# Query and key chunks of sparse attention, cut in quarters over the attention tiles

## The chip, the cores and the metric

One core of a Trainium2 chip. The metric is the device time of one execution in microseconds; the median of three runs of the kernel before is 1286.76 us (1285.74 to 1287.68).

## The reference, cut to what matters

Two transformer blocks on one sequence of 512 tokens with 1024 features. The first (gated mixing, convolution, feed-forward) is not touched. The second has two attentions side by side, and then a feed-forward:

```python
proj = jnp.einsum('bsd,dc->bsc', rmsnorm(x, g_pre_mix), w_in)
(q_a, k_a, v_a, q_i, k_i, w_i, q_d, k_d, v_d) = jnp.split(proj, SPLIT_POINTS, axis=-1)
q_a = apply_rope(q_a.reshape(B, S, DSA_HEADS, HEAD_DIM), cos, sin)
k_a = apply_rope(k_a.reshape(B, S, DSA_HEADS, HEAD_DIM), cos, sin)
...
o_a = dsa_attention(q_a, k_a, v_a, q_i, k_i, w_i)      # 8 heads of 64, each query keeps its top 128 keys
o_d = diff_attention(q1, q2, k1, k2, v_d, lam)         # 4 heads: (softmax(q1 k1) - lam softmax(q2 k2)) v
mix = jnp.concatenate([o_a.reshape(B, S, DSA_W), rmsnorm(o_d, g_diff_sub) * (1.0 - lam_init)], axis=-1)
x = x + rmsnorm(jnp.einsum('bsc,cd->bsd', mix, w_out), g_post_mix)
```

"Sparse attention" is dsa_attention, "differential attention" is diff_attention. The top 128 keys are the same for all eight heads of a query; here they come out of 16 rounds, in each of which the eight largest scores are found and struck out, and become a mask.

## The kernel before, in words

The engines run programs of their own, written out by hand in the order in which each works, and meet at semaphores only. Features lie on partitions, tokens on the free axis.

**Weights.** All weights come from HBM as chunks of 128 x 1024 float32, in one stream (`wstream`, put together in `kernel`, line 1830 on), over four slots. SP reloads a slot when GpSimd has split it (L303). GpSimd splits each chunk into a high part (`high`, L342) and a low part (`low`, L345: a subtraction of two SBUF tensors), when TensorE has done the chunk four before (`chunk_done`). A float32 product is made of three matmuls (`three`, L449 to L452: high by high, high by low, low by high), so a chunk is 8 x 3 matmuls of 128x512 (`chunk_transposed`, L454).

**Tiles.** The attention stage has 48 tiles of 128 queries: tiles 0 to 15 are the four differential heads by four query blocks, tiles 16 to 47 the eight sparse heads by four query blocks. Block tb of a head looks at (tb + 1) x 128 keys, so tiles come in four widths. Each engine has its own `step(n)`. TensorE (L804): scores of tile n+2 (or n+3 in the sparse part) into banks 4 and 5 by turns (`scores`, L726), output pieces, `turn(n)` (L746: transposes of the probabilities), `values(n-1)` (L759). VectorE (L1688): `normalise(n)` (L1666), then `shift(n+2)` (L1651: mask and row extreme). ScalarE (L1121): copy of the turned tile (`keep_turned`, L1098), exp of tile n+2 (L1088), the head's output and its square every fourth tile (`keep_output`, L1109).

**Between the tiles.** The differential heads are normalised by a root over their 128 features. TensorE sums the squares after tiles 5, 9, 13 and 17 (L819), ScalarE takes roots at tiles 9 and 17 (L1136), VectorE builds diagonals (`spread`, L1239) at tiles 10 and 18, and TensorE spreads them over the partitions (`norm_spread`, L537) at the tiles of SPREAD_AT; VectorE then scales the kept head by them (L1698 to L1705). ScalarE makes its high part (HIGH_AT, L1140), GpSimd its low part (L419).

**The sparse queries and keys.** Eight chunks, four of q_a and then four of k_a, are projected from C_QA on. `STEPS_AFTER` (L97) says how many tiles each engine does after each chunk: two after the first, one after each other, so tiles 0 to 8 lie between the chunks, whole chunks each, in banks 0, 1, 2 by turns (L828). Two chunks make a rotary pair (first and second halves of four heads): VectorE's `rope_first` (L1553), `rope_second` (L1563) and `rope_join` (L1568), the last of which adds and subtracts two SBUF tensors. The last pair has a tile between second and join. After each even chunk VectorE does one of the last four top rounds (`top`, L1604), after chunk 6 the mask (L1731). ScalarE moves each finished pair into `qa` or `ka` with eight DMAs in a row (`move_rope`, L1037), after the step of every second chunk (L1162). Nothing but the tiles themselves lies on TensorE from then to tile 21.

**Output pieces.** The second half of the output product, for the differential heads, is cut in 32 pieces of three matmuls (`out2_piece`, L789), one per tile from FILL_FROM = 21 on and two at tiles 26, 30, 34 and 38 (`pieces_at`, L100), in banks 2 and 7. `turn` uses bank 3 in the differential tiles and banks 0 and 3 by turns in the sparse ones.

## Time and profile before

| | us |
|---|---|
| median of three runs | 1286.76 |
| the profiled execution | 1278.78 |
| its span, first to last instruction | 1277.1 |
| TensorE busy in the span | 1204.4 (94%) |
| VectorE busy | 654.9 (51%) |
| GpSimd busy | 703.4 (55%) |
| ScalarE busy | 286.4 (22%) |
| granted TensorE clock, mean over the span | 0.976 of full |

The profile is of one execution. Times on its timeline are us from the span's start. The attention stage runs from about 683 to 862. A matmul's start is what to go by: at a steady rate those of 128x512 start every 0.23 us and are listed with 0.39 us, since they overlap.

### The profile page before, as it was taken

The numbers are of one execution on the slowest core, as the hardware profiler recorded it, in microseconds if no ns is written. First come the engines' busy times: TensorE is split into PE (matmuls) and PEld (weight loads), VectorE is DVE, ScalarE is ACT, GpSimd is POOL, SyncE is SP. The second block draws the span as 40 slices with busy tenths as digits, with TensorE's granted clock in tenths as the row PEclk, the third lists the DMA queues.
The fourth block names the chain that finished last, engine by engine and source line by source line (L and its number), as shares of the span: only waits on it lengthen the run. The fifth ranks groups of instructions, "written<-read, shape, count | busy, mean of one in ns | idle before, by whom it ended". The sixth has DMA issues, their size and how long they took to land.

```text
span 1277.1 us, 15445 instructions
## 1 busy us (share of the span) xinstructions
PE 1204.4 (94%) x5310; PEld 948.4 (74%) x5310; DVE 654.9 (51%) x1011; ACT 286.4 (22%) x553; POOL 703.4 (55%) x421
## 2 busy tenths in 40 slices
PE   7999778999999999999999989998899999999995
PEld 5877556888888888877676755666688888888883
DVE  4996956551015534467996775435755100444114
ACT  5153133220002211110202245444231000221011
POOL 6866336666666666655554421214586666666652
PEclk9999979999999999999999989999899999999997
DMA  6321102333222222224332320001032222323201
GB/s 239 130 83 64 52 31 102 99 99 99 96 91 93 98 99 99 99 91 132 99 99 83 99 83 1 20 31 66 17 132 95 91 93 99 99 99 99 99 17 66
DMA packets 34319, 111.23 MB, mean 87 GB/s; under 512 B 4704, under 2 KB 4832, under 8 KB 34272
## 3 DMA queue, kind: packets, MB, share of 16 engines
q1 hardware_dynamic: 29520, 103.30, 24.1%
q10 hardware_dynamic: 4752, 7.31, 2.1%
q8 instruction: 29, 0.48, 0.2%
q14 instruction: 18, 0.15, 0.0%
HBM read 102.99 MB, written 2.10 MB: 82 GB/s over the span
## 4 chain that ended last, share of the span: by engine, by line
PE 84%; DVE 11%; issue 2%; ACT 1%; ACTq 1%; POOL 1%; DMA 0%; DVEq 0%; POOLq 0%
PE bank L450 24%; PE bank L451 23%; PE bank L452 23%; PE bank L779 2%; PE bank L743 2%; DVE bank L1315 2%; PE bank L481 2%; PE bank L483 2%; PE bank L482 2%; DVE ss L1223 1%; PE bank L540 1%; PE bank L756 1%; DVE work L1595 1%; ACTq L1043 1%; DVE xl L1229 1%
## 5 line engine op out<-in xcount | busy, mean ns | idle before, releaser
L345 POOL TENSOR_TENSOR wl<-raw,wh 128x1024 fp32r<-128x1024 f32 x188 | 457.8, 2435 | 15.7
L342 POOL TENSOR_SCALAR wh<-raw 128x1024 fp32r<-128x1024 f32 x188 | 203.7, 1083 | 459.6 <-PE bank L452 348.6
L450 PE MATMUL bank<-xh,wh 128*128 128x512 f32 x840 | 338.8, 403 | 17.6 <-DVE xl L1229 8.8
L451 PE MATMUL bank<-xl,wh 128*128 128x512 f32 x840 | 330.0, 393 | 0.0
L452 PE MATMUL bank<-xh,wl 128*128 128x512 f32 x840 | 329.9, 393 | 0.0
L450 PE MATMUL bank<-uh,wh 128*128 128x512 f32 x576 | 227.3, 395 | 6.0 <-DVE ul L1338 3.1
L451 PE MATMUL bank<-ul,wh 128*128 128x512 f32 x576 | 224.7, 390 | 0.0
L452 PE MATMUL bank<-uh,wl 128*128 128x512 f32 x576 | 224.7, 390 | 0.0
L450 PEld LDWEIGHTS bank<-xh,wh 128*128 128x128 f32 x840 | 159.3, 190 | 69.6 <-issue 24.5
L452 PEld LDWEIGHTS bank<-xh,wl 128*128 128x128 f32 x840 | 159.3, 190 | 33.9
L451 PEld LDWEIGHTS bank<-xl,wh 128*128 128x128 f32 x840 | 159.7, 190 | 32.5 <-issue 1.4
L1482 DVE TENSOR_TENSOR ul<-tmb,uh 128x512 f32 x64 | 123.7, 1932 | 90.2 <-ACT uh L1017 90.2
L1016 ACT ACTIVATE tmb<-tmp 128x512 f32<-128x512 f32 x64 | 40.5, 633 | 418.6 <-DVE tmp L1479 418.6
L450 PEld LDWEIGHTS bank<-uh,wh 128*128 128x128 f32 x576 | 108.7, 189 | 32.2 <-issue 6.0
L451 PEld LDWEIGHTS bank<-ul,wh 128*128 128x128 f32 x576 | 108.7, 189 | 23.1 <-issue 0.9
L452 PEld LDWEIGHTS bank<-uh,wl 128*128 128x128 f32 x576 | 108.5, 188 | 22.8
L1479 DVE SCALAR_TENSOR_TENSOR tmp<-bank,rb 128x512 f32<-128x512 f32 x64 | 44.1, 690 | 82.1 <-PE bank L452 71.9
L1315 DVE SCALAR_TENSOR_TENSOR bank<-gpad,cols,bank 128x512 f32<-128x512 f32 x108 | 73.2, 752 | 0.0
L1493 DVE TENSOR_TENSOR x<-bank,x 128x512 f32 x8 | 5.5, 692 | 78.1 <-PE bank L452 78.1
L1495 DVE COPY y<-bank 128x512 f32 x8 | 5.5, 692 | 78.1 <-PE bank L452 78.1
L1500 DVE TENSOR_TENSOR y<-bank,y 128x512 f32<-128x512 f32 x8 | 5.5, 692 | 72.3 <-PE bank L452 72.3
L481 PE MATMUL bank<-wh,xh 128*128 128x512 f32 x96 | 39.1, 408 | 3.0 <-DVE tmb L1210 3.0
(217 smaller groups left out, 1151.1 us busy)
## 6 DMA issues: line engine op xcount, KB each, us to landing
raw<-wstream SPq DMA_DIRECT2D x189, 512.0 KB, 3.3
x<-xT SPq DMA_DIRECT2D x8, 256.0 KB, 5.9
out<-x SPq DMA_DIRECT2D x8, 256.0 KB, 2.1
qi<-ropey ACTq DMA_DIRECT2D x16, 64.0 KB, 2.2
qd<-ropey ACTq DMA_DIRECT2D x16, 64.0 KB, 2.5
kd<-ropey ACTq DMA_DIRECT2D x16, 64.0 KB, 2.0
qa<-ropey ACTq DMA_DIRECT2D x16, 64.0 KB, 2.1
ka<-ropey ACTq DMA_DIRECT2D x16, 64.0 KB, 2.1
```

What stands on the lines that cost most here:

```text
L342: nc.gpsimd.tensor_scalar(wh[c][:], raw[c][:], 1.0, 1.0, ALU.mult, ALU.mult).then_inc(high_ready, 1)
L345: nc.gpsimd.tensor_tensor(wl[c][:], raw[c][:], wh[c][:].bitcast(F32), ALU.subtract).then_inc(split_ready, 1)
L450: mm(out, wh_, mh, start=start, stop=False)
L451: mm(out, wh_, ml, start=False, stop=False)
L452: return mm(out, wl_, mh, start=False, stop=stop)
L481: mm(out, xh[:, k, ts], wh[s][:, ws], start=k == 0, stop=False)
L482: mm(out, xh[:, k, ts], wl[s][:, ws], start=False, stop=False)
L483: last = mm(out, xl[:, k, ts], wh[s][:, ws], start=False, stop=k == 7)
L1016: A(tmb[c][:], tmp[c][:], ACT.Square).then_inc(square_ready, 1)
L1315: ins = V.scalar_tensor_tensor(out=out, in0=src, scalar=w, in1=acc, op0=ALU.mult, op1=ALU.add)
L1479: V.scalar_tensor_tensor(out=tmp[c][:], in0=bank[c][:], scalar=0.0, in1=rb[:], op0=ALU.max, op1=ALU.mult).then_inc(evacuated, 1)
L1482: V.tensor_tensor(ul[:, bass.ds(r * 4 + c, 1), :].rearrange("p a n -> p (a n)"), tmb[c][:], uh[:, bass.ds(r * 4 + c, 1), :].rearrange("p a ...
```

## The change

The chunks of q_a and k_a come by groups of four heads: two of q_a, two of k_a, then the other two of each (C_QK). Each chunk is cut in four quarters of six matmuls, and `quarters_at(n)` gives the quarters that TensorE does at the head of its step n: two at tiles 0 to 7, one at tiles 8 to 19, and two at 9, 12, 15 and 18. The chunks use banks 0 and 2 by turns, and a semaphore of their own, `qk_out`, counts VectorE's readings of them. VectorE does rope_first after its step of the tile that ends an even chunk (1, 5, 10, 16), and rope_second and rope_join together after that which ends an odd one (3, 7, 13, 19); the top rounds come after steps 0, 2, 4 and 6, the mask after step 9. ScalarE issues two rotary DMAs after each of four steps, from tiles 4, 8, 14 and 20 on. TensorE asks for the first two pairs' DMAs before the scores of tile 16 and for all before those of tile 32. `turn` alternates banks only from tile 22 on. HIGH_AT goes from tiles 18, 19, 20, 22 to 20 to 23, and the output pieces begin at tile 23 in place of 21, with two at 25, 28, 31, 34, 37 and 40.

```diff
--- before.py
+++ after.py
@@ -67,9 +67,8 @@
 C_KD = C_QD + 4
 C_VD = C_KD + 4
 C_VA = C_VD + 4
-C_QA = C_VA + 4
-C_KA = C_QA + 4
-C_OUT2 = C_KA + 4
+C_QK = C_VA + 4
+C_OUT2 = C_QK + 8
 C_FF2 = C_OUT2 + 8
 CHUNKS = C_FF2 + 4 * FH
 
@@ -79,8 +78,7 @@
 E_P2 = E_FF1 + 2 * FH
 E_VD = E_P2 + 13
 E_VA = E_VD + 4
-E_QA = E_VA + 4
-E_OUT2 = E_QA + 8
+E_OUT2 = E_VA + 4
 E_FF2 = E_OUT2 + 16
 
 
@@ -88,13 +86,34 @@
 
 DIFF_TILES = DIFF_HEADS * TB
 TILES = DIFF_TILES + HEADS * TB
-FILL_FROM = 21
+FILL_FROM = 23
+ALTERNATE_FROM = 22
 
 
 SPREAD_AT = {11: 0, 12: 1, 19: 2, 21: 3}
-HIGH_AT = {18: 0, 19: 1, 20: 2, 22: 3}
+HIGH_AT = {20: 0, 21: 1, 22: 2, 23: 3}
 OUT2_BANKS = (0, 6, 2, 3)
-STEPS_AFTER = (2, 1, 1, 1, 1, 1, 1, 1)
+ROUNDS_AT = (0, 2, 4, 6)
+MASK_AT = 9
+MOVES_FROM = {4: 6, 8: 7, 14: 8, 20: 9}
+
+
+def quarters_at(n):
+
+
+    if n < 0 or n >= 20:
+        return range(0)
+    if n < 8:
+        return range(2 * n, 2 * n + 2)
+    doubled = (9, 12, 15, 18)
+    first = 8 + n + sum(d < n for d in doubled)
+    return range(first, first + 1 + (n in doubled))
+
+
+def turn_bank(n):
+
+    return 0 if n >= ALTERNATE_FROM and n % 2 == 0 else 3
+
 
 
 def pieces_at(n):
@@ -102,7 +121,7 @@
 
     if n < FILL_FROM:
         return range(0)
-    doubled = (26, 30, 34, 38)
+    doubled = (25, 28, 31, 34, 37, 40)
     first = n - FILL_FROM + sum(d < n for d in doubled)
     return range(first, first + 1 + (n in doubled))
 
@@ -276,7 +295,7 @@
         scores_done, shifted, exp_done, probs_ready, turned, pT_ready, pv_done, o_kept = (
             sem("scores_done"), sem("shifted"), sem("exp_done"), sem("probs_ready"), sem("turned"),
             sem("pT_ready"), sem("pv_done"), sem("o_kept"))
-        lam_exp = sem("lam_exp")
+        lam_exp, qk_out = sem("lam_exp"), sem("qk_out")
         ym_gained, y_scaled, y_gained, x4_step = sem("ym_gained"), sem("y_scaled"), sem("y_gained"), sem("x4_step")
         result_step, pool_result, stored = sem("result_step"), sem("pool_result"), sem("stored")
 
@@ -731,9 +750,9 @@
                     for half_moved in rope_moved:
                         pe.wait_ge(half_moved, 16 * 8 * 3)
                     pe.wait_ge(relu_out, 24)
-                if n == DIFF_TILES:
+                if n in (DIFF_TILES, DIFF_TILES + 4 * TB):
                     for half_moved in rope_moved:
-                        pe.wait_ge(half_moved, 16 * 8 * 5)
+                        pe.wait_ge(half_moved, 16 * 8 * (4 if n == DIFF_TILES else 5))
                 q, k = (qd, kd) if diff else (qa, ka)
                 for g in ((2 * h, 2 * h + 1) if diff else (h,)):
                     i = score_tile(n) + (g % 2 if diff else 0)
@@ -747,11 +766,11 @@
 
                 diff, h, tb = tile_of(n)
                 pe.wait_ge(probs_ready, n + 1)
-                if n == DIFF_TILES:
-                    pe.wait_ge(evacuated, E_OUT2)
+                if n == ALTERNATE_FROM:
+                    pe.wait_ge(qk_out, 8)
                 elif n:
-                    pe.wait_ge(pT_ready, n if diff else n - 1)
-                out = bank[3 if diff or n % 2 else 0]
+                    pe.wait_ge(pT_ready, n if n < ALTERNATE_FROM else n - 1)
+                out = bank[turn_bank(n)]
                 for j in range(tb + 1):
                     last = nc.tensor.transpose(out[:, j * P:j * P + P], probs[2 * (n % 3)][:, j * P:j * P + P], ident[:])
                 last.then_inc(turned, 1)
@@ -762,9 +781,7 @@
                 diff, h, tb = tile_of(n)
                 if diff:
                     out, v, cs = bank[1 if h == 3 else 6][:], vd, slice(h * P, h * P + P)
-                    if tb == 0 and h == 3:
-                        pe.wait_ge(evacuated, E_OUT2)
-                    elif tb == 0 and h:
+                    if tb == 0 and 0 < h < 3:
                         pe.wait_ge(o_kept, h)
                 else:
                     pair = h // 2
@@ -793,6 +810,8 @@
                 if k == 0:
                     if o % 2 == 0:
                         pe.wait_ge(split_ready, n + 1)
+                    if o == 0:
+                        pe.wait_ge(qk_out, 8)
                     if o == 1:
                         pe.wait_ge(bc_used, 12)
                     if o >= 2:
@@ -801,8 +820,27 @@
                 if k == 3:
                     last.then_inc(chunk_done if o % 2 else even_out_done, 1)
 
+            def project_quarter(quarter):
+
+                c, q = divmod(quarter, 4)
+                s = (C_QK + c) % SLOTS
+                out = bank[2 * (c % 2)][:]
+                if q == 0:
+                    pe.wait_ge(split_ready, C_QK + c + 1)
+                    if c < 2:
+                        pe.wait_ge(evacuated, E_OUT2)
+                    else:
+                        pe.wait_ge(qk_out, c - 1)
+                for k in (2 * q, 2 * q + 1):
+                    ks = slice(k * P, k * P + P)
+                    last = three(out, wh[s][:, ks], wl[s][:, ks], xh[:, k], xl[:, k], k == 0, k == 7)
+                if q == 3:
+                    last.then_inc(chunk_done, 1)
+
             def step(n):
 
+                for quarter in quarters_at(n):
+                    project_quarter(quarter)
                 if n + 2 <= DIFF_TILES:
                     scores(n + 2)
                 if DIFF_TILES < n + 3 < TILES:
@@ -822,18 +860,8 @@
                     pe.wait_ge(bc_used, 8 + h)
                     norm_spread(8 + h)
 
-            step(-2)
-            step(-1)
-            n = 0
-            for c, steps in enumerate(STEPS_AFTER):
-                pe.wait_ge(split_ready, C_QA + c + 1)
-                pe.wait_ge(evacuated, E_QA + max(c - 2, 0))
-                chunk_transposed((C_QA + c) % SLOTS, bank[c % 3][:], xh, xl)
-                for _ in range(steps):
-                    step(n)
-                    n += 1
-            for m in range(n, TILES + 1):
-                step(m)
+            for n in range(-2, TILES + 1):
+                step(n)
 
 
             def out2(m, ks):
@@ -1034,10 +1062,10 @@
             norm_rb(7, rb2)
 
 
-            def move_rope(g, dst, m):
+            def move_rope(g, dst, m, heads=range(4)):
 
                 act.wait_ge(rope_ready, g + 1)
-                for hh in range(4):
+                for hh in heads:
                     for part in range(2):
                         p0 = 64 * (hh % 2) + 32 * part
                         act.dma_start(dst[p0:p0 + 32, 2 * m + hh // 2], ropey[32 * hh:32 * hh + 32, g % 2, part]
@@ -1104,7 +1132,7 @@
                     act.wait_ge(pv_done, n - 1)
                 else:
                     act.wait_ge(score_step, 24)
-                A(pT[n % 2][:, 0:N], bank[3 if diff or n % 2 else 0][:, 0:N], ACT.Copy).then_inc(pT_ready, 1)
+                A(pT[n % 2][:, 0:N], bank[turn_bank(n)][:, 0:N], ACT.Copy).then_inc(pT_ready, 1)
 
             def keep_output(h):
 
@@ -1149,22 +1177,13 @@
                     act.wait_ge(pv_done, n)
                     A(xh[:, pair], bank[(6, 1)[pair % 2]][:], ACT.Copy).then_inc(xh_ready, 1)
 
-            step(-2)
-            step(-1)
-            n = 0
-            for c, steps in enumerate(STEPS_AFTER):
-                for _ in range(steps):
-                    step(n)
-                    n += 1
-                if c == 7:
-                    step(n)
-                    n += 1
-                if c % 2:
-                    if c == 5:
-                        act.wait_ge(logit_done, 24)
-                    move_rope(6 + c // 2, (qa, ka)[c // 4], c // 2 % 2)
-            for m in range(n, TILES + 1):
-                step(m)
+            for n in range(-2, TILES + 1):
+                step(n)
+                for first, g in MOVES_FROM.items():
+                    if first <= n < first + 4:
+                        if g == 7:
+                            act.wait_ge(logit_done, 24)
+                        move_rope(g, (qa, ka)[g % 2], (g - 6) // 2, range(n - first, n - first + 1))
 
 
             for k in range(KT):
@@ -1550,7 +1569,7 @@
             V.scalar_tensor_tensor(out=tmp[3][64:96, :], in0=b0[64:96, :], scalar=IDX_SCALE, in1=rb[64:96, :],
                                    op0=ALU.mult, op1=ALU.mult).then_inc(evacuated, 1)
 
-            def rope_first(g, n, first):
+            def rope_first(g, n, first, out=evacuated):
 
                 dve.wait_ge(chunk_done, n + 1)
                 if g:
@@ -1558,19 +1577,19 @@
                 else:
                     dve.wait_ge(ki_ready, 1)
                 mul(tmp[0][:], first[:], cosr[:]).then_inc(rope_step, 1)
-                mul(tmb[3][:], first[:], sinr[:]).then_inc(evacuated, 1)
-
-            def rope_second(g, n, second):
+                mul(tmb[3][:], first[:], sinr[:]).then_inc(out, 1)
+
+            def rope_second(g, n, second, out=evacuated):
                 dve.wait_ge(chunk_done, n + 2)
                 mul(tmp[1][:], second[:], sinr[:]).then_inc(rope_step, 1)
-                mul(tmp[2][:], second[:], cosr[:]).then_inc(evacuated, 1)
-
-            def rope_join(g, out0):
+                mul(tmp[2][:], second[:], cosr[:]).then_inc(out, 1)
+
+            def rope_join(g, out0, out=evacuated):
                 if g >= 2:
                     dve.wait_ge(rope_moved[g % 2], 128 * (g // 2))
                 dve.wait_ge(rope_step, 3 * g + 2)
                 V.tensor_tensor(ropey[:, g % 2, 0], tmp[0][:], tmp[1][:], ALU.subtract).then_inc(rope_step, 1)
-                dve.wait_ge(evacuated, out0 + 2)
+                dve.wait_ge(out, out0 + 2)
                 dve.wait_ge(rope_step, 3 * g + 3)
                 V.tensor_tensor(ropey[:, g % 2, 1], tmp[2][:], tmb[3][:], ALU.add).then_inc(rope_ready, 1)
 
@@ -1710,25 +1729,18 @@
                         lows[0] += DIFF_HEADS
                     low_of(pair, bank[(6, 1)[pair % 2]][:])
 
-            step(-2)
-            step(-1)
-            n = 0
-            for c, steps in enumerate(STEPS_AFTER):
-                for _ in range(steps):
-                    step(n)
-                    n += 1
-
-                g = 6 + c // 2
-                if c % 2:
-                    rope_second(g, C_QA + c - 1, bank[c % 3])
-                    if c == 7:
-                        step(n)
-                        n += 1
-                    rope_join(g, E_QA + c - 1)
-                else:
-                    rope_first(g, C_QA + c, bank[c % 3])
+            for n in range(-2, TILES + 1):
+                step(n)
+                for quarter in quarters_at(n):
+                    c = quarter // 4
+                    if quarter % 4 == 3 and c % 2 == 0:
+                        rope_first(6 + c // 2, C_QK + c, bank[0], qk_out)
+                    elif quarter % 4 == 3:
+                        rope_second(6 + c // 2, C_QK + c - 1, bank[2], qk_out)
+                        rope_join(6 + c // 2, c - 1, qk_out)
+                if n in ROUNDS_AT:
                     top(1)
-                if c == 6:
+                if n == MASK_AT:
                     dve.wait_ge(top_step, marks[0])
                     for tb in range(1, TB):
                         N = (tb + 1) * P
@@ -1736,8 +1748,6 @@
                         V.tensor_scalar(work[:, tb, 0:N], work[:, tb, 0:N], TAKEN / 2, NEG, ALU.is_gt, ALU.mult
                                         ).then_inc(top_step, 1)
                     dve.wait_ge(top_step, marks[0] + 3)
-            for m in range(n, TILES + 1):
-                step(m)
             low_of(3, bank[1][:])
 
 
@@ -1830,7 +1840,7 @@
     parts = [glu, natural(v), tiles(u, P), tiles(w_out[:512], 256), tiles(w_out[512:], 256),
              *feed_forward(f["w_ff1"][0], f["w_ff2"][0]),
              tiles(idxk, P), tiles(halves(q_i), P), tiles(halves(q_d), P), tiles(halves(k_d), P), natural(v_d),
-             natural(v_a), tiles(halves(q_a), P), tiles(halves(k_a), P), 
+             natural(v_a), *(tiles(halves(w), P)[2 * g:2 * g + 2] for g in range(2) for w in (q_a, k_a)),
              tiles(f["w_out_2"][0][512:], 256), tiles(f["w_out_2"][0][:512], 256),
              *feed_forward(f["w_up_2"][0], f["w_down_2"][0])]
     cols = [f["norm1_g"], f["norm2_g"], f["final_g"], f["g_pre_mix_2"], f["g_post_mix_2"], f["g_pre_mlp_2"],
```

## Rows read from the trace of the kernel before

**Rows 1.** The profile's page: span, and the chain that ended last by engine.
```profile
span 1277.1 us, 15445 instructions
...
PE 84%; DVE 11%; issue 2%; ACT 1%; ACTq 1%; POOL 1%; DMA 0%; DVEq 0%; POOLq 0%
```

**Rows 2.** Stretches: length; busy TensorE, weight loads, VectorE, ScalarE, GpSimd; clock; DMA; GB/s.
```profile
685.20:786.60 101.40, 90.59 (x446) 64.84 (x445) 75.21 (x219) 39.96 (x109) 32.13 (x19) 0.95 0.23 68
751.60:761.80 10.20, 7.21 (x29) 5.25 (x29) 5.65 (x20) 6.27 (x16) 0.00 (x0) 0.52 0.26 72
786.60:862.00 75.40, 75.40 (x367) 48.27 (x368) 33.06 (x111) 33.72 (x94) 14.31 (x10) 1.00 0.07 22
```

**Rows 3.** Timeline of TensorE: start, us, line, shapes, [idle before, releaser].
```profile
750.22 0.44 PE L756 MATMUL bank<-ident,probs 128*128 128x128 f32 x2 [1.32 <-DVE probs L1681]
...
758.57 1.09 PE L756 MATMUL bank<-ident,probs 128*128 128x128 f32 x4 [1.56 <-ACT tmp L1107]
...
786.58 0.33 PE L756 MATMUL bank<-ident,probs 128*128 128x128 f32 x1 [1.37 <-DVE probs L1686]
```

**Rows 4.** Timeline of TensorE: a tile, the first of a chunk, what follows it.
```profile
708.53 0.70 PE L743 MATMUL bank<-kd,qd 64*128 64x256 f32 x4
...
710.25 0.48 PE L450 MATMUL bank<-xh,wh 128*128 128x512 f32 x1
...
715.89 0.92 PE L743 MATMUL bank<-kd,qd 64*128 64x384 f32 x4
```

**Rows 5.** Timeline of ScalarE, two places.
```profile
706.84 5.69 ACTq L1043 DMA_DIRECT2D qa<-ropey  x8
712.64 0.60 ACT L1107 ACTIVATE tmb<-bank 128x512 f32<-128x512 f32 x1 [8.67 <-issue]
...
787.12 0.61 ACT L1095 ACTIVATE probs<-probs,soft 128x384 f32<-128x384 f32 x1
...
787.72 0.62 ACT L1145 ACTIVATE xh<-rb 128x512 fp32r<-128x512 f32 x1
```

**Rows 6.** Timeline of TensorE: a lone output piece and what follows it.
```profile
794.14 0.50 PE L450 MATMUL bank<-xh,wh 128*128 128x512 f32 x1
...
794.93 0.60 PE L756 MATMUL bank<-ident,probs 128*128 128x128 f32 x4
```

**Rows 7.** Timeline of VectorE, 690 to 788.
```profile
692.99 1.66 DVE L1210 TENSOR_TENSOR soft<-soft,nlam 128x1 f32<-128x1 f32 x1
...
720.96 0.16 DVE L1677 RECIPROCAL soft<-soft 128x2 f32<-128x2 f32 x1
...
721.61 0.48 DVE L1681 SCALAR_TENSOR_TENSOR probs<-probs,soft,probs 128x256 f32<-128x256 f32 x1
724.66 0.69 DVE L1662 CUSTOM_DVE_ANT_0 probs<-bank,mask 128x512 f32<-128x512 f32 x1 [2.56 <-PE bank L743]
...
725.88 0.69 DVE L1210 TENSOR_TENSOR tmp<-bank,cosr 128x512 f32<-128x512 f32 x1
...
727.08 1.47 DVE L1611 MAX8 max<-work 128x8 f32<-128x256 f32 x3
...
730.05 0.16 DVE L1677 RECIPROCAL soft<-soft 128x2 f32<-128x2 f32 x1
...
751.30 0.69 DVE L1572 TENSOR_TENSOR ropey<-tmp,tmp 128x512 f32<-128x512 f32 x1
...
752.70 0.16 DVE L1677 RECIPROCAL soft<-soft 128x2 f32<-128x2 f32 x1
...
784.20 0.75 DVE L1702 SCALAR_TENSOR_TENSOR rb<-rb,diff_gain,bank 128x512 f32<-128x512 f32 x1 [2.27 <-PE bank L540]
...
786.05 0.15 DVE L1685 RECIPROCAL soft<-soft 128x1 f32<-128x1 f32 x1
```

**Rows 8.** Groups of instructions, VectorE, 685 to 786: busy, mean ns, idle.
```profile
L1572 DVE TENSOR_TENSOR ropey<-tmp,tmp 128x512 f32<-128x512 f32 x4 | 6.1, 1534 | 0.0
```

**Rows 9.** Timeline of GpSimd.
```profile
692.29 2.35 POOL L345 TENSOR_TENSOR wl<-raw,wh 128x1024 fp32r<-128x1024 f32 x1
```

## The prediction

> **What bounds the kernel now.** First the page's chain of waits: TensorE carries 84% of the span [rows 1], so a change pays only where TensorE stands idle or runs slow. Then busy time by stretch, around the attention stage. From the first query chunk to the transpose of tile 20 TensorE is busy 90.59 of 101.40 us, so it idles 10.8 us; for 10.2 us of it, in which it is busy 7.21 us, the granted clock is 0.52, so it runs at 1.2 instead of 2.4 GHz and half of the 7.21 us, 3.5 us, is lost [rows 2]. From tile 20 to the last tile it is never idle and at full clock [rows 2]. So 14.3 us (10.8 + 3.5) is all that there is to win, and all of it lies ahead of tile 20. The timeline of TensorE says where: its long waits are those of the transposes for VectorE's probabilities (1.32 and 1.37 us) and one for ScalarE's copy of the turned tile (1.56 us); three of the eleven stand in [rows 3]. Most come after 747.6, when the last query or key chunk is done and tiles 9 to 20 run with no dense work between them; the clock falls there too. Within the chunks one tile costs 1.72 us and a chunk 5.64 us [rows 4], and TensorE does not wait.
>
> **The change, part by part.** The matmuls are the same; they are cut otherwise, and VectorE and ScalarE get their duties at other points.
>
> Removed: all the waits between 685.2 and 786.6, 10.8 us, and the slow stretch, 3.5 us. Everything that waits again is entered below as new. Among the removed is the 1.56 us in which ScalarE was late: it issued eight rotary DMAs in a row (5.69 us for eight, 0.7 each) ahead of the copy of a turned tile [rows 5]. Two per tile put 1.4 us on a tile.
>
> Added by the cutting: TensorE had 8 blocks of chunk work, now 20 (tiles 0 to 19). A piece of three matmuls takes 794.93 - 794.14 = 0.79 us [rows 6], and three of a chunk take 5.64/8 = 0.70 us [rows 4], so entering a block costs about 0.1 us. A whole chunk has 24 matmuls in 5.64 us, and 0.23 us between starts makes 5.5 of it, so there 0.15. I take 0.12: 12 x 0.12 = +1.4 us; the ends are 1.1 and 1.8. The output pieces go from 28 blocks to 26: -0.2. That they begin two tiles later moves two pieces behind, and no more: tiles 23 on are without a gap, so a piece costs the same at either place.
>
> New waits, tiles 0 to 8. Here TensorE does two quarters per tile (2.9 us) and the tile (about 1.6 us: the mean over four widths, estimated from the 1.72 us at one of the wider ones [rows 4]), so 9.0 us for a pair. VectorE's work for a pair: two normalises of about 1.1 (720.96 to the end of the last, 721.61 + 0.48), two shifts of about 0.85 (a pair of 512 wide takes 725.88 - 724.66 = 1.22, of 128 wide a third of it), one round of the top-k, 730.05 - 727.08 = 2.97, and in turn rope_first, 1.20, or rope_second, the same two products, and rope_join, 752.70 - 751.30 = 1.40 [rows 7]. That is 8.1 and 9.5 us. The join is seldom 1.4: its first half takes 1.53 us in the mean of four where the free one takes 0.69 [rows 7, 8], since GpSimd's subtraction runs at that time. So both engines have about 9 us per pair and neither has slack, where before a chunk of 5.64 us and a tile, 7.3 us, stood against 4 to 6 us of VectorE. I walked the queues tile by tile from 685.2. For tile 1 TensorE is ready at 693.0; VectorE shifts tile 2 when its scores are there (689.2 to 690.1), does a round (693.1), and normalises tile 1 by 694.1: wait 1.0. Tile 3: 0.9 (round, then normalise of 512). Tile 5: 0.1. Tile 7: 0.9. Tile 8: 1.3 (behind rope_second and a delayed rope_join). Then VectorE has air, as there is one quarter or two per tile and no more rounds.
>
> At tile 1 it matters which engine is first. The row: a product of a single column took 1.66 us from 692.99, until 694.65, and GpSimd's subtraction ran from 692.29 for 2.35, to 694.64 [rows 7, 9]. In the walk the subtraction of the chunk that follows chunk 0 begins at 693.4, within 0.1 us of the normalise of tile 1; if it is first, tile 1 is ready at 696.4 and the wait is 3.4 in place of 1.0. I take the middle, 2.2, and keep both ends. The Trainium skill (SBUF — State Buffer, "SBUF: two separate sides") says that VectorE with two SBUF inputs and GpSimd share one pair of ports as an exclusive lock, which whoever starts first holds for a whole instruction. This speaks against the change, as it packs the same locks into less time; by that rule the wait is 3.4 or 1.0 and nothing between, and the trace agrees with the lock itself.
>
> Tile 14: rope_second and rope_join of the third pair stand ahead of its normalise: 1.2, the lock's end, 1.4 and 1.25, from 752.8 on, end at 756.8, against TensorE at 755.2: 1.6 us.
>
> Tile 20: the worst place. VectorE at step 19 waits for TensorE's spread matmul, scales the kept head and builds the next diagonal, 786.05 - 784.20 = 1.85 us [rows 7]; with 0.5 for normalise, 2.35. TensorE waited 1.37 us [rows 3], so about 1.0 of it lay beside its scores. Now rope_second (1.2) and rope_join (1.4) of the last pair follow it, ahead of normalise: 1.35 (0.5 less, with the diagonal free of GpSimd) + 1.2 + 1.4 + 0.5 = 4.5, with the hop between engines 4.6, less 1.0: 3.6 us. No quarter and no piece is there to cover it. Tile 22: the same scaling of head 3 had a piece over it and has none: 0.8. ScalarE at tiles 20 to 23 has a copy (0.4), an exp (0.75), the high part of a head (0.6) and two DMAs (1.4), 3.2 us [rows 5], against TensorE's 1.8 to 2.6, so the last high part comes 0.6 us late for the doubled pieces of tile 25. Turns in bank 3 alone to tile 21 now wait for the copy of the tile before, which ScalarE has made by then: 0; without that cover it is some 0.4 each. The new waits on qk_out hold nothing up: the first quarter of a chunk asks for VectorE's reading of the chunk two before, done some two tiles earlier, and the first piece, at tile 23, for the last reading, done ahead of tile 20's normalise; if one were late, all of TensorE's queue would stand behind it. MASK_AT and the moved top rounds cost VectorE what they did. SP reloads and GpSimd splits the same chunks in a new order, each at least four tiles ahead: 0, and if a chunk were late its split, 3.5 us, would show.
>
> Sum: -10.8 - 3.5 + 1.4 - 0.2 + (2.2 + 0.9 + 0.1 + 0.9 + 1.3 + 1.6 + 3.6 = 10.6) + 0.8 + 0.6 = -1.1 us. The profiled execution is 1278.78 us (span 1277.1 and 1.7 around it); the median of the runs, 1286.76, lies 8 us or 0.6% above, and I carry the difference over: 1285.7.
>
> **Rivals.** (1) Forecast: the waits move rather than vanish, 1285.7, within 0.2%, 2.6 us, which is about what a measurement can tell from no change. Chance 0.40. (2) Faster: the walk overstates VectorE. Each of my waits is a small difference of two long queues, and a wait early on shifts what follows; if GpSimd is second at tile 1 (1.0) and the waits of tiles 3 to 8 and 14 are half of what I have, 2.4 for 4.8, it is -1.1 - 1.2 - 2.4 = -4.7: 1282.1. For it: in the chunks of before TensorE shows no waits [rows 4] though VectorE had locks there. Against: per pair it has no slack. Chance 0.38. (3) Slower: the clock falls at tile 20. There TensorE idles 3.6 us and then does only small matmuls up to tile 23. It fell before among small matmuls behind waits of 1.3 to 1.4 us [rows 2, 3], though it held after the 1.37 us of tile 20. If it stays low for 10.2 us as then, and TensorE has work all this while, half of it is lost: -1.1 + 5.1 = +4.0: 1290.8. It decides from about 7.5 us of half clock on. Chance 0.22. That the new order does nothing (the waits come back one for one) is the upper half of (1).
>
> Range: 1280.0 (rival 2, with half of the tile 20 wait, 1.8, gone too and 1.1 for the blocks: -6.8) to 1290.8 (rival 3). The forecast's own range is 1284.2 to 1288.5, by the tile 1 ends (-1.2, +1.2), the block cost and 1 us for waits hidden in modelled durations. Chances: faster 0.38, same 0.40, slower 0.22.
>
> **What would show it.** Quarters in every tile 0 to 19 and no run of small matmuls until 20. A transpose waiting over 3 us on VectorE at tile 20, and about 1 us each at tiles 1, 3, 7, 8 and 14. TensorE's wait in the whole stage near 12 us where it was 10.8, with no slow stretch, or a slow one only after tile 20. ScalarE's DMAs in twos. It is wrong if VectorE's joins do not stand ahead of the late transposes, if the sum of waits is under 8 us (rival 2), or if the clock falls (rival 3).

## The result, and the profile after

Over eight runs each the changed kernel took 1294.55 us (1292.62 to 1301.48) and the kernel before 1286.19 (1279.43 to 1295.96): a ratio of 1.008, interval 1.0042 to 1.0119. It is slower, by 8.4 us between the medians, and above the range that was given. The profiled execution took 1292.97 us where the one of before took 1278.78: 14.2 us apart, more than the medians. That difference matters below ("The base").

The head of the page of the changed kernel, against [rows 1]:

```profile
span 1291.2 us, 15448 instructions
...
PE 1208.8 (94%) x5310; PEld 948.7 (73%) x5310; DVE 661.8 (51%) x1011; ACT 287.2 (22%) x553; POOL 705.1 (55%) x421
```

TensorE has the same 5310 matmuls, and is busy longer. The busy time by stretch says where, against [rows 2]. First stand the two stretches on either side of tile 20's transpose, then two of those with a low clock (columns: stretch, its length, busy time of TensorE, weight loads, VectorE, ScalarE and GpSimd, granted clock, DMA share, GB/s):

```profile
686.50:797.40 110.90, 93.78 (x445) 65.55 (x444) 78.71 (x219) 39.59 (x107) 31.38 (x17) 0.94 0.19 58
722.00:728.50 6.50, 6.50 (x23) 5.53 (x22) 3.12 (x10) 1.79 (x5) 0.00 (x0) 0.50 0.34 103
797.30:803.20 5.90, 5.78 (x17) 3.33 (x17) 1.58 (x7) 3.00 (x8) 1.61 (x2) 0.50 0.15 38
797.40:872.00 74.60, 73.84 (x342) 46.61 (x343) 34.27 (x110) 33.08 (x93) 15.37 (x10) 0.96 0.10 29
```

The first stretch grew from 101.4 to 110.9 us. TensorE idles 110.90 - 93.78 = 17.1 us of it, where it was 10.8: +6.3. Three pieces of it ran at 1.2 GHz, of 3.2, 6.5 and 3.0 us, each at a clock of 0.50 or 0.51 and full of work; half is lost, 6.4 us where it was 3.5: +2.9. By these records the remaining 0.3 of the 9.5 us is all that the twelve added blocks can have cost. Behind tile 20 a fourth such piece (5.8 us busy at 0.50) loses 2.9 us, and 0.7 us is idle: from tile 20's transpose to that of the last tile it is 74.8 us against 71.4. The stage was also entered 1.3 us later than before (686.5 for 685.2), ahead of anything that the change touches; two profiles of one and the same kernel differ there by 2.2 and 2.5 us, so this is scatter. 9.5 + 3.4 + 1.3 = 14.2.

The idle time is that of the transposes. The long waits on TensorE's timeline (start, duration, what, and in brackets the idle time ahead and who ended it), for tiles 1, 3, 5, 7, 8, 10, 11 and 14, and then 20 and 22, against [rows 3]:

```profile
697.47 0.47 PE L775 MATMUL bank<-ident,probs 128*128 128x128 f32 x2 [3.01 <-DVE probs L1700]
708.68 0.66 PE L775 MATMUL bank<-ident,probs 128*128 128x128 f32 x4 [1.46 <-DVE probs L1700]
721.57 0.66 PE L775 MATMUL bank<-ident,probs 128*128 128x128 f32 x2 [2.98 <-DVE probs L1700]
735.27 0.66 PE L775 MATMUL bank<-ident,probs 128*128 128x128 f32 x4 [1.47 <-DVE probs L1700]
739.71 0.33 PE L775 MATMUL bank<-ident,probs 128*128 128x128 f32 x1 [0.87 <-DVE probs L1700]
748.44 0.55 PE L775 MATMUL bank<-ident,probs 128*128 128x128 f32 x3 [0.40 <-DVE probs L1700]
753.32 0.66 PE L775 MATMUL bank<-ident,probs 128*128 128x128 f32 x4 [1.87 <-DVE probs L1700]
769.00 0.55 PE L775 MATMUL bank<-ident,probs 128*128 128x128 f32 x3 [1.71 <-DVE probs L1700]
...
797.42 0.47 PE L775 MATMUL bank<-ident,probs 128*128 128x128 f32 x1 [3.38 <-DVE probs L1705]
...
805.09 0.55 PE L775 MATMUL bank<-ident,probs 128*128 128x128 f32 x3 [0.74 <-DVE probs L1705]
```

Tiles 1 and 5 wait 3 us. What VectorE and GpSimd did just before, against [rows 9]:

```profile
694.73 2.41 POOL L364 TENSOR_TENSOR wl<-raw,wh 128x1024 fp32r<-128x1024 f32 x1
694.97 2.44 DVE L1700 SCALAR_TENSOR_TENSOR probs<-probs,soft 128x256 f32<-128x256 f32 x1
...
718.86 2.38 POOL L364 TENSOR_TENSOR wl<-raw,wh 128x1024 fp32r<-128x1024 f32 x1
719.08 2.44 DVE L1700 SCALAR_TENSOR_TENSOR probs<-probs,soft,probs 128x256 f32<-128x256 f32 x1
```

Both times GpSimd's subtraction starts 0.2 us ahead of the last, two-input step of the normalise, which takes 0.48 us when free [rows 7], and here lasts until the subtraction is done. Tile 20's place is as the walk had it: the kept head, the diagonal, both products, both halves of the join, and only then the normalise (VectorE's timeline):

```profile
793.02 0.75 DVE L1721 SCALAR_TENSOR_TENSOR rb<-rb,diff_gain,bank 128x512 f32<-128x512 f32 x1 [5.02 <-PE bank L559]
793.69 0.68 DVE L1262 TENSOR_TENSOR diag<-ident,rn 128x512 f32<-128x512 f32 x1
794.29 0.68 DVE L1229 TENSOR_TENSOR tmp<-bank,sinr 128x512 f32<-128x512 f32 x1
794.89 0.68 DVE L1229 TENSOR_TENSOR tmp<-bank,cosr 128x512 f32<-128x512 f32 x1
795.49 0.68 DVE L1591 TENSOR_TENSOR ropey<-tmp,tmp 128x512 f32<-128x512 f32 x1
796.27 0.69 DVE L1594 TENSOR_TENSOR ropey<-tmp,tmb 128x512 f32<-128x512 f32 x1
...
797.08 0.29 DVE L1705 TENSOR_SCALAR probs<-probs,soft 128x128 f32<-128x128 f32 x1
```

### The profile page after: what moved, and what is told of

Same layout as the page of the kernel before. It is cut to its first block, busy times and chain, and to the rows that moved or that the text cites. A ratio compares the mean times of both kernels' runs of the same rounds, so it can differ in the third digit from the quotient of the medians.

```text
span 1291.2 us, 15448 instructions
## 1 busy us (share of the span) xinstructions
PE 1208.8 (94%) x5310; PEld 948.7 (73%) x5310; DVE 661.8 (51%) x1011; ACT 287.2 (22%) x553; POOL 705.1 (55%) x421
## 4 chain that ended last, share of the span: by engine, by line
PE 82%; DVE 13%; issue 3%; POOL 1%; ACT 1%; ACTq 0%; DMA 0%; DVEq 0%; POOLq 0%
PE bank L469 23%; PE bank L471 22%; PE bank L470 22%; PE bank L796 2%; PE bank L762 2%; DVE bank L1334 2%; PE bank L500 2%; PE bank L502 2%; PE bank L501 2%; DVE ss L1242 2%; PE bank L559 1%; PE bank L775 1%; DVE work L1614 1%; PE bank L538 1%; DVE diag L1262 1%
```

## The experiments

The ratios are to the kernel before, measured beside each. To compare the stage between profiles I cut 680 to 872 us into windows of 2 us and summed, for each, the idle time of TensorE and its busy time times (1 - granted clock), called lost here. It takes in the ends of the stage, so it is a little above the sums of the text. The column "us" is the time of the profiled execution, to which idle and lost belong; the ratio is that of all the runs.

```
profile                      us      ratio   idle  lost
before, prediction's run  1278.78       -    11.4   3.6
before, run again         1285.93  1.0009    10.5   8.6
changed                   1292.97  1.008     18.4   9.4
changed, run again        1290.50  1.0099    18.4   9.3
throw-aways at 4 tiles    1290.18  1.005      9.9   3.3
GpSimd held               1291.73  1.0044    14.5  10.9
last join later           1297.77  1.0104    18.0  11.3
two rounds ahead          1288.34  1.0028    12.9  14.7
joins placed earlier      1284.17  1.0075    15.6   7.6
three remedies together   1271.24  0.993      6.7   0.0
the same again            1269.96  0.9921     6.8   0.0
 without the hold         1279.10  0.9996    12.0   4.5
 DMAs by eights           1280.58  0.9971    10.6   4.8
before, DMAs by twos      1289.57  1.0037     8.1  19.3
before, two rounds ahead  1287.95  0.999     11.5   8.8
before, throw-aways       1279.72  1.0023     7.2   1.3
changed, whole chunks     1311.67  1.0213    25.3  21.0
```

Idle hardly differs between two profiles of one kernel (11.4 and 10.5, 18.4 and 18.4, 6.7 and 6.8). Lost does: 3.6 and 8.6 in the kernel before. And a profile need not be typical: those of "GpSimd held" and "two rounds ahead" are of executions 6.7 and 5.3 us above their medians, that of "joins placed earlier" is 7.0 below its own. Of a single profile, idle can be trusted more than lost.

**As it is, once more.** The changed kernel, no edit.

> The changed kernel as it is, beside the others of this group, as their common measure: 1.006 to 1.010 of the time of before by every theory; a new profile has the same waits to 0.1 us (VectorE's queue fixes them), with the slow stretches behind them, but not always the same ones.

1291.25 us, 1.0099 (1.0068 to 1.013). All ten waits are back within 0.03 us (3.01, 1.45, 2.97, 1.46, 0.87, 0.39, 1.87, 1.74, 3.38, 0.74), and the clock fell behind tiles 1, 5, 14 and 20 again. The waits belong to the program.

**Does the clock fall because TensorE stands still?** Throw-away matmuls, into a bank that the tile writes later, fill the wait; nothing else changes.

```diff
+WARM_AT = {1: 3, 5: 3, 14: 1, 20: 3}
-                pe.wait_ge(probs_ready, n + 1)
...
+                for _ in range(WARM_AT.get(n, 0)):
+                    mm(out[:], ones[:], mask[:], start=True, stop=True)
+                pe.wait_ge(probs_ready, n + 1)
```

> TensorE does throw-away matmuls (ones by mask, into the bank that the transposes then overwrite) while it waits for VectorE: three at tiles 1, 5 and 20, one at tile 14. Theory A (clock): in the profile of the changed kernel the clock fells to half four times, about 20 us in all, each time right behind one of these waits; some 9 us are lost by it. Then the waits stay, the slow stretches behind them go, and this kernel is 7 to 10 us faster than the changed one, at or below the time of before. Theory B (waits): the waits themselves are the loss; then it is no faster than the changed kernel (0 to +1 us). Theory C (cutting): the loss comes of the chunks cut in 20 blocks; also no change here.

1288.38 us, 1.005 (1.0024 to 1.0076). The waits at the four tiles shrank to 0.25, 0.21, 0.65 and 0.61 us, and no low clock follows those of tiles 1, 5 and 14. It follows the untouched 1.88 us of tile 11 (749 to 753 us), and stands at 801 to 804, behind a wait of 1.30 us at tile 22. So the falls at these tiles hang on the standstills. A standstill alone does not decide it: tile 11's 1.87 us had no fall behind it in the changed kernel. It bought less than expected: the lost time fell by 6.1 us in the profiles, and the ratio by 0.3 to 0.5%, 4 to 6 us.

**GpSimd's lock.** GpSimd splits a chunk only once the normalise that it used to meet is done.

```diff
+LATE_AFTER = (2, 4, 6, 8, 11, 15, 17, 21)
+                done = n - SLOTS - C_QK
+                if 0 <= done < 8:
+                    pool.wait_ge(probs_ready, LATE_AFTER[done])
```

> GpSimd waits with the split that follows each finished query or key chunk until VectorE has normalised the tile of that moment, so its subtraction no longer runs beside that normalise. Theory A (lock, then clock): at tiles 1 and 5 the last operation of normalise took 2.44 us instead of about 0.5, up to the end of GpSimd's subtraction; without it the waits of 3.0 us there become about 1 us, the two slow stretches behind them go, and the kernel is 7 to 9 us faster than the changed one. Rival (VectorE is simply too full in tiles 0 to 8): the waits at 1 and 5 stay above 2 us and the time within 2 us of the changed kernel.

1285.02 us, 1.0044 (1.0014 to 1.0075). Tile 1 waits 1.05 us, which is the low end of the prediction, and tile 5 not at all; tiles 2 and 4 now wait 0.80 and 0.91, and tile 8 waits 2.23 where it was 0.87. That the hold moved a collision to tile 8 is likely but not shown. In its profile the clock falls behind tiles 8 and 14, and is low from 791 to 808, behind tile 20's untouched 3.38 us.

**Tile 20.** The last products and join are put behind step 20.

```diff
-MOVES_FROM = {4: 6, 8: 7, 14: 8, 20: 9}
+MOVES_FROM = {4: 6, 8: 7, 14: 8, 21: 9}
-                for quarter in quarters_at(n):
+                for quarter in quarters_at(n) if n < 19 else (31,) if n == 20 else ():
```

> The last rope_second and rope_join follow step 20 of VectorE in place of step 19, and ScalarE's last eight DMAs begin a tile later. Theory: the transpose of tile 20 waits about 1.4 us in place of 3.4, the clock holds there, and the kernel is 3 to 5 us faster than the changed one. Rival: the wait only moves to tile 21 or 22, and the time is within 1 us of the changed kernel.

1295.23 us, 1.0104 (1.0066 to 1.0143). The wait moved, as the rival had it; the timeline of this kernel, tiles 20, 21 and 22:

```profile
798.13 0.33 PE L775 MATMUL bank<-ident,probs 128*128 128x128 f32 x1 [0.79 <-DVE probs L1705]
802.53 0.44 PE L775 MATMUL bank<-ident,probs 128*128 128x128 f32 x2 [2.64 <-DVE probs L1705]
806.45 0.90 PE L775 MATMUL bank<-ident,probs 128*128 128x128 f32 x3 [0.22 <-DVE probs L1705]
```

**VectorE's load.** Two of the four top-k rounds are done ahead of the stage, where TensorE's wait at 683 us is 1.48 us instead of 0.53.

```diff
-ROUNDS_AT = (0, 2, 4, 6)
+ROUNDS_AT = (2, 6)
-            top(TOPK // 8 - 1 - 4)
+            top(TOPK // 8 - 1 - len(ROUNDS_AT))
```

> Two of the four late top rounds, those after steps 0 and 4, are done before the attention tiles, where VectorE stood idle for 6.65 us waiting for TensorE. Theory (the round, 2.97 us, ahead of normalise 1 and 5 is what makes them late, and late enough to meet GpSimd's subtraction): the 3.0 us waits at tiles 1 and 5 fall below 0.5 us, both slow stretches go, 8 to 10 us faster than the changed kernel. Rival (VectorE pays the rounds elsewhere): the stage begins later by up to 3 us, and it is 3 to 6 us faster only.

1283.09 us, 1.0028 (1.0004 to 1.0052), the lowest of the single remedies, though not clear of the hold's interval. The 3 us waits of tiles 1 and 5 are gone, the rest stay (1.34, 1.47, 0.88, 0.40, 1.87, 1.71, 3.38). The profile has two short stretches at a low clock, behind tiles 11 and 14, and a long one behind tile 20, from 784 on:

```profile
784.00:808.00 24.00, 22.14 (x59) 12.80 (x60) 8.39 (x29) 7.45 (x20) 5.05 (x4) 0.52 0.10 25
```

**The joins alone.** The join of the third pair goes behind step 14, the last one ahead of the scaling in step 19.

```diff
-MOVES_FROM = {4: 6, 8: 7, 14: 8, 20: 9}
+MOVES_FROM = {4: 6, 8: 7, 15: 8, 20: 9}
+                if n == 19:
+                    rope_second(9, C_QK + 6, bank[2], qk_out)
+                    rope_join(9, 6, qk_out)
...
+                if n == 14:
+                    rope_join(8, 4, qk_out)
```

> The changed kernel with only the joins placed otherwise: rope_second and rope_join of the last pair ahead of the scaling of head 2 in step 19, in VectorE's idle 5 us, and the third pair's join after step 14. Theory: the waits at tiles 14 and 20 (1.7 and 3.4 us) fall below 1 and 1.7 us and the slow stretches behind them go, those at 1 and 5 stay: 4 to 7 us faster than the changed kernel. Rival: GpSimd's subtraction, which runs beside this join, makes it end as late as before; then within 1 us.

1291.17 us, 1.0075 (1.0037 to 1.0113): tile 14 waits 0.26 and tile 20 2.06 us, together 2.8 less. The time can't be told from the changed kernel's.

**All three together.** These joins, the two rounds, and a hold fitted to the new order.

```diff
+LATE_AFTER = (10, 5, 18, 10, 12, 16, 18, 21)
+                    pool.wait_ge(shifted if done in (0, 2) else probs_ready, LATE_AFTER[done])
-ROUNDS_AT = (0, 2, 4, 6)
+ROUNDS_AT = (2, 6)
```

> All of the remedies together: two top rounds ahead of the stage, GpSimd's splits held back to places where VectorE uses no second SBUF input, rope_second and rope_join of the last pair ahead of the scaling of head 2 in step 19 (where VectorE stood idle 5 us), the join of the third pair after step 14. Theory A: the change's idea, cover in all tiles 0 to 19, was sound and its loss came of VectorE's queue alone; then the waits at tiles 1, 5, 14 and 20 fall below 1.5 us each, the clock falls at most once, and the kernel ends 8 to 13 us below the changed one, 0 to 5 us below before. Rival: the 20 blocks and the gap of tiles 20 to 22 cost enough that it stays 2 us or more above before.

1271.8 us, 0.993 (0.9904 to 0.9956). It beats both kernels. Its busy time by stretch:

```profile
684.00:777.00 93.00, 87.64 (x446) 60.64 (x447) 67.19 (x203) 39.83 (x107) 26.20 (x16) 1.00 0.20 63
777.00:860.00 83.00, 82.16 (x398) 54.00 (x398) 35.45 (x111) 34.81 (x96) 21.87 (x14) 1.00 0.12 39
```

TensorE's work to tile 20 takes 87.64 us for 446 matmuls (0.3 of it lies behind the start of tile 20's transpose), and the clock is full in both stretches. TensorE's wait at tile 20 is 0.79 us:

```profile
776.60 0.33 PE L780 MATMUL bank<-ident,probs 128*128 128x128 f32 x1 [0.79 <-DVE probs L1710]
```

> The fast combination once more, on this group's chip: 0.990 to 0.996 of before again if the gain is real, with under 7 us of TensorE idle in the stage and at most one slow stretch; a slow stretch would cost it 2 to 4 us.

1271.69 us, 0.9921 (0.9894 to 0.9949): the same.

**That version without its hold.** `LATE_AFTER`'s wait is left out; the rest stays.

```diff
-                if 0 <= done < 8:
-                    pool.wait_ge(shifted if done in (0, 2) else probs_ready, LATE_AFTER[done])
```

> The fast combination without the hold on GpSimd: its splits start as soon as a chunk is done, as in the changed kernel. By the theory that the lock only hurts where VectorE is late anyway, the waits at tiles 1 and 5 stay under 0.5 us as the rounds are no longer ahead of them, the last join at step 19 meets the subtraction (a wait of about 2 us at tile 20, as in the kernel with the joins alone), and it is 1 to 4 us slower than the combination. By the rival that the hold carries the gain, 6 us or more slower.

1282.34 us, 0.9996 (0.9973 to 1.0019): the hold is worth 0.7 to 0.8%, 9 us, of which 5.3 is idle time and 4.5 low clock in the profiles. Waits of 2.42 and 2.06 us are back at tiles 11 and 20, with the clock low behind them.

**That version with its rotary DMAs by eights.**

```diff
-                    if first <= n < first + 4:
+                    if n == first:
-                        move_rope(g, (qa, ka)[g % 2], (g - 6) // 2, range(n - first, n - first + 1))
+                        move_rope(g, (qa, ka)[g % 2], (g - 6) // 2, range(4))
```

> The fast combination with the rotary DMAs in rows of eight again, at the first of the four tiles. By the theory that two per tile matter once every tile is short (5.7 us of DMA issue against 3 to 4.4 us per tile): the copy of a turned tile comes 2 to 3 us late at tiles 5, 9, 16 and 21, TensorE waits for ScalarE, and it is 3 to 8 us slower than the combination. By the rival that the DMA order is a detail: within 1.5 us.

1278.59 us, 0.9971 (0.9942 to 1.0): by the ratios (0.9921 and 0.993) 0.4 to 0.5% slower, 5 to 6 us, though the intervals overlap a little. One wait for VectorE at tile 11 is 2.80 us, and waits of 0.5 to 0.9 for ScalarE appear.

**The kernel before with DMAs by twos.**

```diff
+                for first, g in MOVES_FROM.items():
+                    if first <= n < first + 4:
...
+                        move_rope(g, (qa, ka)[(g - 6) // 2], g % 2, range(n - first, n - first + 1))
```

> The kernel before with one part of the change: ScalarE issues its rotary DMAs two per tile in place of eight in a row. The wait of 1.56 us for ScalarE's copy goes. By the theory that this part is harmless or good: 0 to 3 us faster than before. By a rival, that DMAs landing later hold up the scores of tile 16, slower by 1 to 2 us.

1286.02 us, 1.0037 (1.0008 to 1.0065): a little slower. The idle time fell by 3.3 us, ScalarE's wait with it, and the time rose. In its profile, of an execution 3.6 us above the median, the clock is low for three stretches, the longest from 769 to 797:

```profile
769.00:797.00 28.00, 28.00 (x82) 16.91 (x81) 9.78 (x33) 12.47 (x29) 3.79 (x3) 0.50 0.00 0
```

The waits just ahead of it are 0.83 us (766) and 0.18 us (769), far shorter than those of the changed kernel with a fall behind them. Why the clock falls here is open.

**The kernel before with the two rounds ahead.**

```diff
-            top(TOPK // 8 - 1 - 4)
+            top(TOPK // 8 - 1 - 2)
-                        top(1)
+                    if c in (2, 6):
+                        top(1)
```

> The kernel before with two of the four late top rounds ahead of the stage, the remedy alone without the change. By the theory that the remedies need the change (before, a chunk of 5.64 us hid each round already), within 2 us of before. By the rival that the fast combination owes its time to them and not to the cut chunks, 4 us or more faster than before.

1282.65 us, 0.999 (0.9961 to 1.0018): nothing. That whole chunks cover VectorE's rounds in the old order fits this; the lone exception, tile 1's 1.43 us, did not move.

**The kernel before, not touched.** Is the prediction's profile typical of it?

> The kernel before as it is, for a second profile of it. The prediction's sum was made against an execution of 1278.8 us, 8 us under the median. Theory E: its waits are the same in every execution (11.4 us of TensorE idle in the stage), and what differs is the clock, in the stage and in the stages around it; a profile near 1285 us would show a mean clock of 0.967 to 0.972 and more or longer slow stretches. A profile near 1277.5 us again would show the 0.976 of the first and settle nothing on where.

1284.73 us, 1.0009 (0.9983 to 1.0035). Its profile is of an execution of 1285.93 us. Idle time is 0.9 us less than in the prediction's (tile 10 waits 2.00 for 1.43, tile 20 0.79 for 1.37), but the clock is low in two long stretches and a short one (two shown):

```profile
756.50:766.20 9.70, 6.98 (x25) 4.56 (x25) 4.46 (x17) 5.23 (x13) 0.00 (x0) 0.50 0.22 55
783.20:790.20 7.00, 7.00 (x22) 3.88 (x21) 1.80 (x6) 5.16 (x11) 2.21 (x2) 0.52 0.00 0
```

Lost is 8.6 us where it was 3.6. The stretch at 783.2 begins with no wait over 0.2 us in the 5 us ahead of it. Most executions of this kernel fall into groups near 1277.5 us (mean clock 0.976) and 1285 us (0.967 to 0.971); the prediction's profile is of the first.

**The kernel before, with throw-aways** ahead of the transposes of tiles 1, 9 to 13 and 20.

```diff
+WARM_AT = {1: 1, 9: 1, 10: 1, 11: 1, 12: 1, 13: 1, 20: 1}
```

> The kernel before with one throw-away matmul ahead of the transposes of tiles 1, 9 to 13 and 20, where TensorE waits 1.3 to 1.6 us for VectorE. Runs of before fall in two groups, near 1277.5 and near 1285.5 us. Theory D: the upper group is the same kernel with one more or one longer slow stretch among the small matmuls of tiles 9 to 22; then here nearly all runs lie in one group, at 1274 to 1278, and the profile shows no slow stretch in the stage. Rival: the groups come from another stage; then both stay.

1286.84 us, 1.0023 (0.9995 to 1.0052). Lost is 1.3 us in the profile, which is of the fastest execution, and still nothing is won. The two groups stayed (1279.7 to 1282.4, 1285 to 1291). Inconclusive: the throw-aways also cost time. At tile 11 the first of them waited 2.75 us for ScalarE's copy, where the transposes had waited 1.56.

**Is cutting the chunks at fault?** Whole chunks in the new order.

```diff
+    whole = (1, 3, 5, 7, 10, 13, 16, 19)
+    return range(4 * whole.index(n), 4 * whole.index(n) + 4) if n in whole else range(0)
```

> The changed kernel with its eight chunks whole, at the tiles where their last quarter was (1, 3, 5, 7, 10, 13, 16, 19): eight blocks in place of twenty, all else the same. If the cutting itself costs (0.12 us a block, or more), 1.4 us less on TensorE. Theory A says that the waits matter more: tiles without cover between the chunks wait for VectorE as before, and VectorE's late normalises at 1 and 5 are hidden or not by where the chunk stands; 3 us faster to 3 us slower than the changed kernel. Faster by over 4 us would say that the cutting was the fault.

1306.57 us, 1.0213 (1.0183 to 1.0244), slower than with quarters by 1.1 to 1.3%, 15 us above the changed kernel's second set of runs (1291.25), with seven of its waits at 1.9 to 3.4 us. The quarters are the good part of the change.

## Why the prediction was wrong

**Two terms of the sum failed: "-3.5" for the half clock, with no term for its return, and "10.6" for the new waits to tile 20, which measured 17.1.** Against the profile that the sum was built on, its -1.1 became 14.2 us, 15.3 too few, and the terms account for it: 9.3 for the clock, 6.5 for the waits, 1.3 for the later entry; less 1.1 for the blocks, 0.6 for the wait at tile 25, which did not come, and 0.1 at tile 22.

**The clock.** The sum held it full through all the new waits, and only rival 3 put a fall behind one of them, tile 20. The profile shows four, behind tiles 1, 5, 14 and 20, 18.6 us in all at 1.2 GHz: 3.2 + 6.5 + 3.0 + 5.8, half lost, 9.3 us. The throw-aways show that the standstills bring it at tiles 1, 5 and 14 (behind tile 20 they moved it to the next wait). So rival 3's mechanism was the right one, and its size and places were not: four short stretches instead of one of 10 us. Even its 1290.8 us was too low.

**Waits to tile 20: 17.1 us, not 10.6.** Mechanism right, places partly so.
- Tile 1: 3.0, for a middle of 2.2 between the ends 1.0 and 3.4. GpSimd was first. Holding it gave 1.05, so both ends were true alternatives, and no run stood at the middle. By the Trainium skill (SBUF — State Buffer, "SBUF: two separate sides") whoever starts first keeps the ports for a whole instruction; the trace agrees, 2.44 us beside 2.41.
- Tile 5: 3.0, for 0.1. The largest single error, 2.9 us: the walk priced the lock on a normalise at tile 1 alone, though the same meeting returns with the next chunks. Hold or fewer rounds remove it. The evidence was there: the prediction read that "TensorE does not wait" within the chunks, but the profile of before has a wait of 1.44 us at tile 1 (695.50), right behind the lock of its own [rows 7, 9].
- Tiles 10 and 11: 0.4 and 1.9, which the walk left out because "VectorE has air". The air was there, but not at tile 11.
- Tiles 3, 7, 8 and 14: 1.5, 1.5, 0.9 and 1.7, for 0.9, 0.9, 1.3 and 1.6. At tiles 3 and 7 a meeting of another kind adds some 0.65 us (last section).
- Tile 20: 3.38, for 3.6, and tile 22 0.74, for 0.8: both right, and the timeline shows the order that was argued.

**Blocks:** about 0.3 us for twelve, not 1.4, so some 0.03 us an entry, not 0.12. This is a remainder of modelled durations; the kernel of all three remedies, at full clock, leaves 0.2 (87.3 us to tile 20's transpose, against 90.59 - 3.5 = 87.1).

**DMAs by twos:** right that ScalarE's wait goes. That it needs the other parts to pay is what the pair of kernels suggests: 0.4% slower on the kernel before, 0.4 to 0.5% faster in the repaired one. In the first the loss is low clock (19.3 us lost in its profile), whose cause is open.

**The base.** The sum was built on the 1278.78 us execution and carried 8 us over to the median. The two profiles of that kernel lie 7.2 us apart, with 5.0 more of low clock in this stage (8.6 less 3.6) and 0.9 less idle. So such an execution has more to win than the 14.3 us named as all there is, and the offset was no constant that a change leaves alone. It also decides what the clock is held to have cost. Against the first profile the change lost 14.2 us, 7.0 of it idle and 5.8 low clock (18.4 less 11.4, 9.4 less 3.6). Against the second it lost 7.0 us, and nearly all is idle: 7.9, with 0.8 of low clock. The new waits are the part that both comparisons show. The medians, 8.4 us apart, lie nearer the second, but they mix executions of several clocks on both sides.

**A slip:** the upper end of the forecast's own range comes to 1288.3 by its terms, not 1288.5; nothing hangs on it.

**The rival "faster"** needed half of each wait gone. None of the single remedies does it; all three do, with the waits up to and at tile 20 at 0.17, 1.05, 1.22, 0.56, 0.40, 0.94, 0.23 and 0.79 us, 5.4 us in sum.

Left open: why the clock falls in some executions of the same program and not in others, why it fell behind waits of 0.2 us in two profiles of the old order, and how the gain splits among the three remedies. Alone, hold, rounds and joins give 0.4 to 0.6%, 0.5 to 0.7% and 0.1 to 0.2% (too little to tell from none) over the changed kernel (by its two ratios), together 1.5 to 1.8%; the intervals are too wide to say whether they add or help one another.

## What to carry to other kernels

Spreading dense work over more steps removes standstills only where the engine that feeds TensorE has slack in every step; where both carry the same time per step, each collision shows at once, and can be paid twice, as idle time and as half clock behind it. Price a long wait (in the changed kernel the falls stood behind waits of 1.7 to 3.4 us, in others behind 1.3 us and less too) together with the low clock that may follow it, and look for every place where a lock can return, not only the first. Don't build a sum on one execution if the medians lie elsewhere: see first what differs between the two.

## What was not expected of the hardware

The prediction knew the lock from GpSimd's subtraction of two tensors. Its split into the high part, an operation of one input, holds up VectorE's two-input step too. At tile 3 the 512 wide step ran from 707.23 to 708.63, 1.40 us, where the same form took 0.75 us in the repaired kernel. GpSimd's split ran until 708.09, and the step ended 0.54 us after it:

```profile
706.79 1.30 POOL L361 TENSOR_SCALAR wh<-raw 128x1024 fp32r<-128x1024 f32 x1 [9.66 <-PE bank L471]
707.23 1.40 DVE L1700 SCALAR_TENSOR_TENSOR probs<-probs,soft 128x512 f32<-128x512 f32 x1
```

With dense chunks behind it the low clock of the changed kernel ended after 3.0 to 6.5 us. Between small matmuls of the late tiles it ended after 6 us behind tile 20 there, and lasted 17, 24 and 28 us in three other kernels, although TensorE was busy for 15.44, 22.14 and all 28 of them. And executions of the same program differ by 8 us, 0.6%; the two that were profiled have nearly the same waits.
